# Nine groups of TensorE transposes replaced by 32x32 block turns on VectorE and small SBUF-to-SBUF DMAs in a two-layer hybrid decoder kernel

## The reference, cut to what matters

```python
for l in range(DEPTH):
    h = rms_norm(x, attn_norm[l])          # norm 2l   (counted from 0)
    p = h @ w_in[l]                         # 2048 -> 4672
    ... three mixers ...
    x = x + mixed @ w_o[l]
    h = rms_norm(x, ffn_norm[l])            # norm 2l+1
    gate, up = jnp.split(h @ w_gate_up[l], 2, axis=-1)
    x = x + (silu(gate) * up) @ w_down[l]
```

## Time and profile before

| | |
|---|---|
| median of 3 runs | 2353.47 us (2352.15 to 2355.67) |
| profiled execution, first to last instruction (span) | 2351.5 us |
| TensorE busy | 2324.1 us, 99% |
| VectorE busy | 1331.0 us, 57% |
| ScalarE busy | 1103.5 us, 47% |
| share of the DMA engines' time taken by SyncE's queue | 47.9% |

### The profile page before, as it was taken

How to read it: one execution, slowest core, us unless ns; L and a number is a source line. 1 busy time by engine, 2 the same in 40 slices (tenths; PEclk the granted TensorE clock), 3 DMA queues, 4 the chain that set the end, 5 groups by cost and what they waited for, 6 DMA issues and landing times.

```text
span 2351.5 us, 33396 instructions
## 1 busy us (share of the span) xinstructions
PE 2324.1 (99%) x13481; PEld 1924.8 (82%) x13481; DVE 1331.0 (57%) x1420; ACT 1103.5 (47%) x1362; POOL 55.1 (2%) x58
## 2 busy tenths in 40 slices
PE   8999999999999999999999999999999999999999
PEld 7888688888888888888888886888888888888887
DVE  5686676545445445445557857765454454454454
ACT  6554745544443344444445547454444433444433
POOL 0000110000000000000000002100000000000000
PEclk9999999999999999999999999999999999999999
DMA  7453305555555555554554532044555555555554
GB/s 299 166 184 130 122 21 178 181 195 194 182 195 182 194 196 193 184 194 181 193 184 152 194 115 102 29 171 180 196 189 186 193 184 194 197 191 185 192 184 141
DMA packets 59519, 407.04 MB, mean 173 GB/s; under 512 B 6608, under 2 KB 6704, under 8 KB 13200
## 3 DMA queue, kind: packets, MB, share of 16 engines
q1 hardware_dynamic: 58720, 401.66, 47.9%
q0 software_dynamic: 688, 3.78, 0.5%
HBM read 403.32 MB, written 2.10 MB: 172 GB/s over the span
## 4 chain that ended last, share of the span: by engine, by line
PE 93%; DVE 5%; issue 1%; ACT 0%; DMA 0%; DVEq 0%; SPq 0%; ACTq 0%
PE psum L1475 28%; PE psum L1477 28%; PE psum L1476 28%; PE psum L1669 2%; PE psum L1917 1%; PE psum L2004 1%; PE psum L1764 1%; PE psum L1570 1%; PE psum L1509 1%; DVE arena L1211 1%; DVE arena L1284 0%; DVE arena L1292 0%; DVE small L1194 0%; DVE arena L1188 0%; DVE arena L1178 0%
## 5 line engine op out<-in xcount | busy, mean ns | idle before, releaser
L890 DVE TENSOR_TENSOR w_lo<-raw,w_hi 128x1024 fp32r<-128x1024 f32 (+2 forms) x752 | 901.3, 1205 | 843.9 <-ACT w_hi L451 836.8
L451 ACT ACTIVATE w_hi<-raw 128x1024 fp32r<-128x1024 f32 (+2 forms) x752 | 782.0, 1044 | 1071.8 <-PE psum L1477 1070.2
L1475 PE MATMUL psum<-w_hi,hT_hi 128*128 128x512 f32 (+2 forms) x2128 | 821.6, 386 | 3.1 <-DVE w_lo L890 3.1
L1477 PE MATMUL psum<-w_hi,hT_lo 128*128 128x512 f32 (+2 forms) x2128 | 816.4, 384 | 0.0
L1476 PE MATMUL psum<-w_lo,hT_hi 128*128 128x512 f32 (+2 forms) x2128 | 816.3, 384 | 0.0
L1475 PEld LDWEIGHTS psum<-w_hi,hT_hi 128*128 128x128 f32 x2128 | 399.7, 188 | 81.8 <-DVE w_lo L890 2.4
L1477 PEld LDWEIGHTS psum<-w_hi,hT_lo 128*128 128x128 f32 x2128 | 399.6, 188 | 78.5
L1476 PEld LDWEIGHTS psum<-w_lo,hT_hi 128*128 128x128 f32 x2128 | 399.8, 188 | 76.4
L1475 PE MATMUL psum<-w_hi,act_hi 128*128 128x512 f32 x872 | 340.4, 390 | 0.0
L1477 PE MATMUL psum<-w_hi,act_lo 128*128 128x512 f32 x872 | 339.4, 389 | 0.0
L1476 PE MATMUL psum<-w_lo,act_hi 128*128 128x512 f32 x872 | 339.3, 389 | 0.0
(11 more groups left out here) (319 smaller groups left out, 1194.7 us busy)
## 6 DMA issues: line engine op xcount, KB each, us to landing
raw<-stream_dram SPq DMA_DIRECT2D x360, 1024.0 KB, 4.8
raw<-stream_dram SPq DMA_DIRECT2D x16, 512.0 KB, 3.7
raw<-stream_dram SPq DMA_DIRECT2D x8, 768.0 KB, 4.3
raw<-stream_dram SPq DMA_DIRECT2D x8, 640.0 KB, 3.8
x<-x_in_dram SPq DMA_DIRECT2D x4, 512.0 KB, 9.2
lor<-lora_dram POOLq DMA_DIRECT2D x2, 832.0 KB, 10.3
con<-consts_dram POOLq DMA_DIRECT2D x1, 1648.0 KB, 11.4
out_dram<-x SPq DMA_DIRECT2D x3, 512.0 KB, 7.3
```

The lines of the kernel that those rows point to most:

```text
L451: nc.scalar.activation(w_hi[:, q % HALF_RING, 0:2 * w], raw[:, j % 4, hf * 2 * w:(hf + 1) * 2 * w], ACT.Copy).then_inc(hi_done, 1)
L890: tt(w_lo[:, q % HALF_RING, 0:2 * w], raw[:, j % 4, hf * 2 * w:(hf + 1) * 2 * w], w_hi[:, q % HALF_RING, 0:2 * w].bitcast(F32), SUB).then_ ...
L1475: mm(o, a_hi, w_hi[:, r, cols], start=(k == 0), stop=False)
L1477: last = mm(o, a_lo, w_hi[:, r, cols], start=False, stop=(k == n_k - 1))
```

## The change

For norms 1, 2 and 3 the first three chunks (c = 0, 1, 2: `by_dma`) are no longer transposed by TensorE. That is nine chunks in the kernel. Directly behind `add_x`, VectorE turns the 32 x 32 blocks of the chunk in place on their grid (`x_turn_blocks`: two instructions of 128 x 512, `x` to `x_blocks`, the first 1024 columns of the tensor `gain`). After the split of the third slot ScalarE issues 16 DMAs (`x_move`), each of 32 partitions x 256 elements (32 KB), which put block (b, q) of the grid at (q, b) in `x_moved` (the other half of `gain`). `x_hi` and `x_lo` read `x_moved` in place of PSUM; `x_lo` does so in eight instructions of 128 x 128 in place of four of 128 x 256. Norm 0 and the fourth chunk of each norm stay as they were. Four semaphores of the rotary tables are merged to two, with the same order of work.

```diff
+        x_blocks = gain[:, 0:2 * CH]
+        x_moved = gain[:, 2 * CH:4 * CH]
+        X_MOVES = (P // 32) ** 2
...
+        def by_dma(n, c):
+            return n > 0 and c < 3
+        def moved(n, c):
+            return 3 * (n - 1) + c + 1
...
+            def x_move(n, c):
+                act.wait_ge(S("x_blocks_turned"), moved(n, c))
+                act.wait_ge(S("hT_ready"), 4 * n + c)
+                for q in range(P // 32):
+                    for b in range(P // 32):
+                        act.dma_start(x_moved[32 * q:32 * q + 32, 256 * b:256 * b + 256],
+                                      x_blocks[32 * b:32 * b + 32, 256 * q:256 * q + 256]).then_inc(S("x_moved"), 16)
             def x_hi(n, c):
-                act.wait_ge(S("x_turned"), 4 * n + c + 1)
+                if by_dma(n, c):
+                    act.wait_ge(S("x_moved"), 16 * X_MOVES * moved(n, c))
+                    m4 = x_moved.rearrange("p (b k t e) -> p k t b e", b=4, k=4, t=TT)
+                    for k in range(4):
+                        g = n * KT + 4 * c + k
+                        last = nc.scalar.activation(hT_hi[:, 4 * c + k, :].rearrange("p (t b e) -> p t b e", t=TT, b=4),
+                                                    m4[:, k], ACT.Copy, scale=gain_col[:, g:g + 1])
+                    last.then_inc(S("hT_hi_ready"), 1)
+                    return
+                act.wait_ge(S("x_turned"), turned_at(n, c))
...
+                    if n > 4 and n % 4 == 2:
+                        x_move(2 * l + 1, n // 4 - 1)
                     if n > 4 and n % 4 == 3:
                         x_hi(2 * l + 1, n // 4 - 1)
...
+            def x_turn_blocks(n, c):
+                for t in range(TT):
+                    out4 = x_blocks.rearrange("p (q k t e) -> p t k q e", q=4, k=4, t=TT)[:, t]
+                    in4 = x[:, t, c * CH:(c + 1) * CH].rearrange("p (k q e) -> p k q e", k=4, q=4)
+                    last = nc.vector.transpose(out4, in4)
+                vs(last, "x_blocks_turned", moved(n, c))
...
                     if c and n % 4 == 2:
                         add_x(s4o, 5 if c == 1 else 4 * c, c - 1, 12 * l + c)
+                        x_turn_blocks(2 * l + 1, c - 1)
...
-                    if c and j == 1:
-                        x_turn(2 * l + 1, c - 1)
...
-                            if makes_norm and c and j == 1:
-                                x_turn(2 * l + 2, c - 1)
```

More of the change, by code:

```diff
@@ L299, in added, with turned_at @@
             return 12 * ((n - 1) // 2) + (4 if n % 2 else 12) - 3 + c
+        def by_dma(n, c):
+            return n > 0 and c < 3
+        def moved(n, c):
+            return 3 * (n - 1) + c + 1
+        def turned_at(n, c):
+            return c + 1 if n == 0 else 4 + n
         def x_turn_bank(n, c):
@@ L388, in _ @@
                 pool.wait_ge(row_in, 32 * (l + 1))
-                pool.wait_ge(S("cs_ready"), 2)
+                pool.wait_ge(S("tables_on_act"), 2)
                 cos, sin = cs[:, 0, :, :], cs[:, 1, :, :]
@@ L460, in tables @@
                 for k in range(2):
-                    act.wait_ge(S("angle_ready"), k + 1)
+                    act.wait_ge(S("tables_on_dve"), k + 1)
                     nc.scalar.activation(cs[:, k, :, :], small[:, 64 * k + 8:64 * k + 72].rearrange(
-                        "p (t n) -> p t n", t=TT), ACT.Sin).then_inc(S("cs_ready"), 1)
-                act.wait_ge(S("lb_shifted"), 1)
-                nc.scalar.activation(small[:, 144:152], small[:, 144:152], ACT.Exp).then_inc(S("lb_exp"), 1)
-            def x_hi(n, c):
-                act.wait_ge(S("x_turned"), 4 * n + c + 1)
+                        "p (t n) -> p t n", t=TT), ACT.Sin).then_inc(S("tables_on_act"), 1)
+                act.wait_ge(S("tables_on_dve"), 3)
+                nc.scalar.activation(small[:, 144:152], small[:, 144:152], ACT.Exp).then_inc(S("tables_on_act"), 1)
+            def x_move(n, c):
[5 more added lines that the diff above has]
+                                      x_blocks[32 * b:32 * b + 32, 256 * q:256 * q + 256]).then_inc(S("x_moved"), 16)
+            def x_hi(n, c):
+                if by_dma(n, c):
[8 more added lines that the diff above has]
+                act.wait_ge(S("x_turned"), turned_at(n, c))
                 if n == c == 0:
@@ L850, in _ @@
                             turned_hi(pairs - 1, pair0)
+                        if makes_norm and j > pairs and j % pairs == 2:
+                            x_move(2 * l + 2, j // pairs - 1)
                         if makes_norm and j > pairs and j % pairs == 3:
@@ L900, in x_lo @@
                 dve.wait_ge(S("hT_hi_ready"), 4 * n + c + 1)
+                if by_dma(n, c):
+                    m4 = x_moved.rearrange("p (b k t e) -> p k t b e", b=4, k=4, t=TT)
+                    for k in range(4):
+                        g = n * KT + 4 * c + k
+                        for t in range(TT):
+                            hi, lo = (z[:, 4 * c + k, t * P:(t + 1) * P].rearrange("p (b e) -> p b e", b=4)
+                                      for z in (hT_hi, hT_lo))
+                            last = stt(lo, m4[:, k, t], gain_col[:, g:g + 1], hi.bitcast(F32), MUL, SUB)
+                    last.then_inc(S("hT_ready"), 1)
+                    return
                 for k in range(4):
@@ L945, in tables @@
                 v(stt(co, ang, -1.0, ang, MUL, MAX))
-                vs(ts(co, co, -1.0, float(np.pi / 2), MUL, ADD), "angle_ready", 1)
-                dve.sem_inc(S("angle_ready"), 1)
+                vs(ts(co, co, -1.0, float(np.pi / 2), MUL, ADD), "tables_on_dve", 1)
+                dve.sem_inc(S("tables_on_dve"), 1)
                 dve.wait_ge(par_in, 16)
@@ L952, in tables @@
                 v(tt(small[:, 144:148], lb0, small[:, 136:140], SUB))
-                vs(tt(small[:, 148:152], lb1, small[:, 136:140], SUB), "lb_shifted", 1)
-                dve.wait_ge(S("lb_exp"), 1)
+                vs(tt(small[:, 148:152], lb1, small[:, 136:140], SUB), "tables_on_dve", 3)
+                dve.wait_ge(S("tables_on_act"), 3)
                 v(tt(small[:, 136:140], small[:, 144:148], small[:, 148:152], ADD))
@@ L1440, in _ @@
                                 add_x(s4f, pairs * c, c - 1, 12 * l + 4 * (n + 1) + c)
+                                if makes_norm:
+                                    x_turn_blocks(2 * l + 2, c - 1)
                             split_lo(s4f, pairs * c + j)
```

## The result

| | before | changed |
|---|---|---|
| runs in one comparison, median | 2354.57 us (2352.15 to 2355.80, 4 runs) | 2382.40 us (2380.38 to 2387.99, 4 runs) |
| ratio, 95% interval | | 1.0122 [1.0108, 1.0136] |
| span of the profiled execution | 2351.5 us | 2379.6 us |

The change made the kernel slower by 1.2%, 28 us. The forecast was 2346.0 us with a range up to 2361. The rival on the other side, bursts of issues that cost what they cost at the start, is what came, and it cost more than the 2364 us that this rival had.

The account below looks back on a forecast made before the run. TensorE, busy 99% of the span, was taken to bound the kernel. Nine transpose groups saved 8.0 us, all else hidden; rounded to -7.5 for waits at the edges, 2353.5 - 7.5 = 2346.0 us, range 2344 to 2361.

Parts of the forecast that it names:

- The rival on the other side: Sixteen issues in a row on ScalarE take 0.55 us or more each, TensorE waits in all nine places; 2364 us; chance 0.23.
- Nine groups of transposes, 0.89 us each: Six groups at `w_o`, three at layer 0's down projection leave TensorE's list, saving 8.0 us.
- The rival that TensorE's transposes were hidden: Removing TensorE's transposes changes nothing in the time; no chance to speak of.
- Block turns of 0.71 us, hidden: VectorE's two 128 x 512 instructions behind the addition take 1.42 us and do not delay TensorE.
- `x_lo` about 2.3 us, hidden: Eight 128 x 128 instructions replace four taking 1.66 us; about 2.3 us, at most 3.3, off TensorE's list.
- `x_hi` 1.55 us: The same four instructions of 256 columns, now read from SBUF, take 1.55 us, off TensorE's list.
- Landings of 2.1 to 4.8 us, and no cost of the traffic: The last of 16 small DMAs lands in 2.5 us; 0.5 MB more per chunk beside the weights costs nothing.
- The limits M = 417.1 and 394.45: Latest trace times (us) for ScalarE to finish 16 issues before TensorE waits: 417.1 in seven chunks, 394.45 in two.
- regular chunk: Seven of nine chunks; issues start at 408.95, and one issue may cost up to 0.51 us.
- tight one: First chunk of each `w_o`, two of nine; issues start at 389.0 after ScalarE's copies, one may cost 0.34 us.
- The price of an issue, T = 0.35: One DMA issue holds ScalarE 0.35 us, taken from SyncE's rows on a running stream.
- The two rules of the Trainium skill: One prefers TensorE for 128 x 128 transposes, giving the sum the wrong sign; 50 ns dispatch gives 0.8 us for 16 issues.

Follow-up runs that it names:

- The two kernels whose bursts fit: Changed kernel with eight of sixteen issues per chunk, 2345.55 us; changed kernel with SyncE issuing and `x_hi`, squares and `x_lo` one slot later, 2345.03 us.

## Why the prediction was wrong

By its own steps:

- **Nine groups of transposes, 0.89 us each: right.** The two kernels whose bursts fit gained 7.9 and 8.3 us in their medians, and from slot to slot a group was 0.91 us. The rival that TensorE's transposes were hidden is refuted.
- **Block turns of 0.71 us, hidden: right.** They took 0.69 us in the median, 0.71 at most, scattered output and all; two of them stand as 1.30 us at 386.51.
- **`x_lo` about 2.3 us, hidden: right.** Eight took 2.19 us. **`x_hi` 1.55 us: nearly.** It took 1.69 to 1.71 from SBUF, hidden in the slack.
- **Landings of 2.1 to 4.8 us, and no cost of the traffic: right.** The median was 2.3 us, and 1/32 of the bytes gave the same time. Nowhere in the changed kernel does `x_hi` wait for them.
- **The limits M = 417.1 and 394.45: right.** With T = 0.64 (a burst of 10.3 us) they give a loss of 2.1 us in a regular chunk and 4.8 in a tight one; the trace has 2.3 and 4.9. The prediction read no rows at the down projection and took its chunks as regular, and that holds too: bursts of 11.81, 11.30 and 11.12 us less the slack of 417.1 - 408.95 = 8.15 are 3.7, 3.2 and 3.0, and TensorE lost 3.75, 3.23 and 3.05. Twelve issues, 7.8 us, passed in the regular chunks and failed in the tight ones, as the two limits say.
- **The price of an issue, T = 0.35: wrong, and this is the step that failed.** It was 0.61 us. The prediction had the right rows in hand, the issues in a row at SyncE's start, 0.43 to 0.66 us, and set them aside as a cold start of larger transfers. It took the price of one issue alone on a running stream. Neither the size nor the start made the difference: an issue of 1 KB costs 0.61 us as well, in the middle of the kernel. The source and the issue ahead do, on ScalarE: alone 0.51 from SBUF, in a row 0.61, and from device memory 0.37 and 0.41 at the least. All of these are above T = 0.34, where the tight chunks begin to lose.
- **What was not in the sum.** At T = 0.66 it had +19 us at most, and +28 came. At T = 0.61 it gives +12, and with the measured lengths of the bursts, about 0.64 us an issue and more at the down projection, +20. The issues at the down projection were longer than those at `w_o`, 11.1 to 11.8 us for sixteen, and cost three chunks about 1 us more each. And TensorE's clock halves behind most of the longer waits, 6.8 us. I had priced a wait at its own length.

The two rules of the Trainium skill come out thus. The trace shows 0.51 to 0.61 us for an issue from SBUF to SBUF. "DMA: Bandwidth & Descriptors" (Anatomy of one DMA) gives its 50 ns of dispatch for a DMA that GpSimd issues. The prediction put that figure on ScalarE, where the measured price is ten times as high; no run here moves the blocks from GpSimd. "VectorE: DVE Perf Modes" (Rules for kernel authors) says to transpose 128 x 128 on TensorE where a result in PSUM will do. Read as a forecast of the time, it has the sign of the change as it was made (1.0122) and the wrong one for the same exchange with the issues on SyncE and their reader a slot later (0.9964), where TensorE, the engine without slack, is spared 0.89 us a chunk and VectorE and SyncE have room.

What stays open: why some issues at the down projection take 0.9 to 2.1 us, on ScalarE and on SyncE, and the 2 us of the median in the kernel that issues four at a time. Not tried: issues on GpSimd, and the same exchange for the transposes that the change left on TensorE.

## What to carry to other kernels

Price a DMA issue like an instruction of the engine that issues it, by the row nearest in kind (in a row or alone, from SBUF or from device memory), not by the bytes. A burst must fit into that engine's slack at its place. The slack is a threshold: past it every microsecond of the burst was a microsecond of TensorE's here, and behind the longer waits its clock cost more. Issue bursts from an engine whose list nobody waits for, and move the reader of their data as many slots down as the burst and its last landing last. Here the first alone gave back 24 of 37 us, and both together turned 28 us of loss into 8 of gain. Where the rows of a prediction disagree by a factor of two and the sign hangs on it, the answer is the row that shares the most conditions, and the sum should be made with it.

## What the hardware showed that I had not expected

- An issue from SBUF to SBUF holds the issuing engine 0.51 us alone and 0.61 (ScalarE) in a row, the same from 1 KB to 128 KB and from 16 to 128 partitions. On SyncE the 144 had a median of 0.59.
- No instruction of ScalarE starts while its queue issues: 10.3 us without one, at 46% busy over the span. One that had started before goes on.
- Behind a wait of 4.7 us TensorE runs for about 4 us at a granted clock of 0.50, half its full clock, and behind one of 3.6 us at the down projection 1.4 us were lost in the same way. Behind 2.9 us (the changed kernel at 1185, third chunk of the down projection) the clock did not fall, nor behind 2.15 us (at 424.7), and behind 2.19 us (twelve issues, at 397) it fell and cost 1.4 us. So the length of the last wait alone doesn't decide it; what else does, no run here tells apart.
- Some issues take far longer than the rest: up to 1.7 us on ScalarE (2.1 with twelve issues) and up to 1.5 on SyncE at the down projection, and one of 1.2 on SyncE at `w_o`.
